# Attention's token sums moved into the slots of the convolution norm, and two plain projection slots turned into seven-product slots

## The reference, cut to what matters

```python
n = rms_norm_2(h, mix_norm_g[l])
proj = n @ w_in[l]                       # q k v, index heads, xr, yg, cv (2 x 1024), gt (3 x 1024)
attn = dsa_attention(q, k, v, qi, ki, wi)
rnn  = rg_lru_branch(xr, yg, ...)
cnv  = silu(layer_norm(causal_depthwise_conv(a * sigmoid(g), dw_w, dw_b), ln_g, ln_b))   # 31 taps
g_attn, g_rnn, g_conv = split(sigmoid(gt), 3)
merged = g_attn * (attn @ w_o_attn) + g_rnn * (rnn @ w_o_rnn) + g_conv * (cnv @ w_o_conv)
h = h + merged @ w_out
# then the feed-forward half of the layer
```

## Time and profile before

| | |
|---|---|
| timed runs | 1715.67, 1718.28, 1719.57 us; median 1718.28 us |
| profiled execution | 1715.31 us, span 1713.5 us, mean granted TensorE clock 0.989 |
| busy share of the span | PE 97%, PEld 86%, DVE 66%, POOL 39%, ACT 32% |
| DVE busy from 700 to 800, 1200 to 1300, 1300 to 1400 us | 81%, 88%, 91% |
| slots 34 to 45, first layer | about 767 to 855 us |
| slots 34 to 45, second layer | about 1389 to 1474 us |

### The profile page before, as it was taken

The page is one execution under the profiler, slowest core; times in us unless marked ns, Lnnn a source line. Parts: engine busy times, 40 slices in busy tenths (PEclk is TensorE's granted clock), DMA queues, the critical chain, the costliest instruction groups (busy, mean ns, idle before and its releaser), DMA issues.

```text
span 1713.5 us, 36091 instructions
## 1 busy us (share of the span) xinstructions
PE 1662.7 (97%) x14758; PEld 1475.4 (86%) x14758; DVE 1136.8 (66%) x2047; ACT 556.5 (32%) x1255; POOL 660.5 (39%) x581
## 2 busy tenths in 40 slices
PE   5999998999999999999999999999999999999999
PEld 3777657999889988878889999989888889999999
DVE  5647155665378889995757664368888977576743
ACT  3233463444343444424130100233554314220100
POOL 1534103553045342114636554165122027446552
PEclk9999996999999999999999999999999999999999
DMA  9333200000544434333435444543343343444543
GB/s 383 117 113 123 74 1 2 4 4 4 199 147 136 160 124 148 124 122 124 151 121 197 152 163 160 166 148 126 125 171 124 135 150 131 160 164 170 173 160 111
DMA packets 53379, 225.71 MB, mean 132 GB/s; under 512 B 5088, under 2 KB 29024, under 8 KB 29280
## 3 DMA queue, kind: packets, MB, share of 16 engines
q1 hardware_dynamic: 53216, 223.40, 37.4%
HBM read 222.34 MB, written 1.05 MB: 130 GB/s over the span
## 4 chain that ended last, share of the span: by engine, by line
PE 86%; DVE 7%; ACT 2%; DVEq 2%; DMA 1%; issue 1%; ACTq 0%; SPq 0%
PE PS L742 17%; PE PS L785 17%; PE PS L1052 15%; PE PS L1076 8%; PE PS L2552 5%; PE PS L2664 3%; DVE arena L1474 2%; PE PS L2073 2%; PE PS L2086 2%; PE PS L724 1%; PE PS L2761 1%; PE PS L902 1%; PE PS L865 1%; PE PS L1016 1%; DMA ring<-stream_dram 1%
## 5 line engine op out<-in xcount | busy, mean ns | idle before, releaser
L785 PE MATMUL PS<-arena,ring 128*128 128x272 f32 (+1 forms) x1600 | 374.1, 388 | 0.9 <-DVE arena L1698 0.5
L785 PEld LDWEIGHTS PS<-arena,ring 128*128 128x128 f32 x1600 | 298.8, 190 | 57.9 <-issue 7.0
L1918 POOL TENSOR_TENSOR arena<-ring 128x512 f32<-128x512 f32 x50 | 72.5, 1449 | 447.2 <-DMA ring<-stream_dram 397.1
L1474 DVE SCALAR_TENSOR_TENSOR arena<-arena,par 128x272 f32<-128x272 f32 (+1 forms) x480 | 236.3, 550 | 7.3 <-issue 0.4
L742 PE MATMUL PS<-arena,ring 128*128 128x136 f32 (+1 forms) x1600 | 209.6, 279 | 2.3 <-ACT arena L1162 2.0
L742 PEld LDWEIGHTS PS<-arena,ring 128*128 128x128 f32 x1600 | 199.6, 190 | 9.6 <-ACT arena L1162 2.8
L742 PE MATMUL PS<-arena 128*128 128x136 f32 (+1 forms) x1200 | 155.5, 281 | 4.4 <-DVE arena L1579 3.9
L1052 PE MATMUL PS<-arena 128*128 128x136 f32 (+1 forms) x1280 | 152.1, 277 | 0.0
L742 PEld LDWEIGHTS PS<-arena 128*128 128x128 f32 x1200 | 146.8, 192 | 6.0 <-DVE arena L1735 2.6
L1052 PEld LDWEIGHTS PS<-arena 128*128 128x128 f32 x1280 | 148.7, 191 | 0.0
L1052 PE MATMUL PS<-arena,ring 128*128 128x136 f32 (+1 forms) x960 | 116.1, 277 | 0.0
(11 more groups left out here) (416 smaller groups left out, 2950.5 us busy)
## 6 DMA issues: line engine op xcount, KB each, us to landing
ring<-stream_dram SPq DMA_DIRECT2D x185, 1024.0 KB, 4.9
ring<-stream_dram SPq DMA_DIRECT2D x32, 512.0 KB, 4.3
ring<-stream_dram SPq DMA_DIRECT2D x16, 384.0 KB, 3.5
arena<-x_dram SPq DMA_DIRECT2D x1, 2048.0 KB, 8.3
cst<-const_dram SPq DMA_DIRECT2D x1, 1080.0 KB, 6.7
out_dram<-H SPq DMA_DIRECT2D x4, 256.0 KB, 3.8
cst<-const_dram SPq DMA_DIRECT2D x1, 912.0 KB, 12.2
arena<-stream_dram SPq DMA_DIRECT2D x1, 512.0 KB, 11.1
```

The lines of the kernel that those rows point to most:

```text
L785: last = mm(PS[:, 2 * (j % 2) + f, nw], w[:, k, P * f:P * f + P], src[:, k, nw], start=k == 0, stop=k == KD - 1)
L1474: stt(CVG[:, c, NQ], CVA[:, c, j + Q0:j + T2], dw_w[l][:, c, j:j + 1], CVG[:, c, NQ], ALU.mult, ALU.add)
L1918: g.tensor_tensor(to[:, 0], w21, w22, ALU.add).then_inc(L["summed"], 1)
```

## The change

`CONV_SUM_J` becomes 35 in both layers, and `ATT_SUM_J` 36. Slots 36 and 37 are added to `MIXED`. The four attention sums are split: two in VectorE's slot 36 and two in its slot 37, behind the links of the norm chain that now stand there, and TensorE's waits for them are split likewise. In the first layer the one convolution step of slot 35 goes to slot 34. The norm chain starts one slot earlier in the first layer and two in the second; the attention sums come one slot later in the first and three in the second.

```diff
-CONV_SUM_J, ATT_SUM_J = (36, 37), (35, 33)
+CONV_SUM_J, ATT_SUM_J = 35, 36
-MIXED = [*range(2, 8), 9, 11, 12, 15, 18, 21, 24, 27, 35, *range(OA_J, OC_J + 3), *range(WO_J + 1, MIXES)]
+MIXED = [*range(2, 8), 9, 11, 12, 15, 18, 21, 24, 27, 35, 36, 37, *range(OA_J, OC_J + 3), *range(WO_J + 1, MIXES)]
...
-              for late in ({27: 4, 28: 8, 29: 3, 30: 7, 31: 5, 32: 3, 33: 4, 34: 4, 35: 1},
+              for late in ({27: 4, 28: 8, 29: 3, 30: 7, 31: 5, 32: 3, 33: 4, 34: 5},
...
                     product_g(j)
...
+                    if j == OA_J:
+                        pe.wait_ge(L["att_halves"], B["att_halves"] + 3)
...
                     product_c(j)
+                    if j == OA_J + 1:
+                        pe.wait_ge(L["att_halves"], B["att_halves"] + 4)
...
-                if j == ATT_SUM_J[l]:
+                if j == ATT_SUM_J:
                     dve.wait_ge(L["o_kept"], B["o_kept"] + len(R))
-                    x = AT.rearrange("p (k e) t -> p k e t", e=2)
-                    token_sums(v, x[:, :, 0], x[:, :, 1], TATT, n0, n1).then_inc(L["att_halves"], 1)
+                    tt(sums[0], even[..., n1], even[..., n0], ALU.subtract).then_inc(L["att_halves"], 1)
+                    tt(sums[2], odd[..., n1], even[..., n1], ALU.subtract).then_inc(L["att_halves"], 1)
+                if j == ATT_SUM_J + 1:
+                    dr()
+                    tt(sums[1], odd[..., n1], sums[0], ALU.subtract).then_inc(L["att_halves"], 1)
+                    dr()
+                    tt(sums[3], odd[..., n0], sums[1], ALU.subtract).then_inc(L["att_halves"], 1)
```

More of the change, by code:

```diff
@@ L1291, in scalar_layers @@
                     copy_a(j)
-                    if j == CONV_SUM_J[l] + 1:
+                    if j == CONV_SUM_J + 1:
                         square(0)
-                    if j == CONV_SUM_J[l] + 4:
+                    if j == CONV_SUM_J + 4:
                         conv_silu(1).then_inc(L["conv_out"], 1)
@@ L1397, in scalar_layers @@
                     open_branch(GTS[0][:, 4:8, NQ], GTC_J + 4, True)
-                if j == CONV_SUM_J[l] + 1 and j not in MIXED:
+                if j == CONV_SUM_J + 1 and j not in MIXED:
                     square(0)
                     square(1).then_inc(L["conv_sq"], 1)
-                if j == CONV_SUM_J[l] + 2:
+                if j == CONV_SUM_J + 2:
                     act.wait_ge(L["conv_sq_sum"], B["conv_sq_sum"] + 1)
                     inverse_root(TQ[:, 0, NQ], PS[:, 5, NQ], D, L["conv_root"])
-                if j == CONV_SUM_J[l] + 3:
+                if j == CONV_SUM_J + 3:
                     conv_silu(0)
@@ L1710, in vector_layers @@
             done = 0
+            heads_of = AT.rearrange("p (k e) t -> p k e t", e=2)
+            even, odd, sums = heads_of[:, :, 0], heads_of[:, :, 1], [TATT[:, i, :, 0:nh] for i in range(4)]
             for j in range(1, WO_J):
@@ L1719, in vector_layers @@
                         ).then_inc(L["conv_cent"], 1)
-                if j == CONV_SUM_J[l] + 2:
+                if j == CONV_SUM_J + 2:
                     dve.wait_ge(L["conv_sq"], B["conv_sq"] + 1)
                     add_tiles(v, CSUM[:, 1, NQ], CSQ[:, :, NQ], CSQ[:, 0:4, NQ]).then_inc(L["conv_sq_in"], 1)
-                if j == CONV_SUM_J[l] + 3:
+                if j == CONV_SUM_J + 3:
                     dve.wait_ge(L["conv_root"], B["conv_root"] + 1)
                     tt(CVG[:, :, NQ], CVG[:, :, NQ], over(TQ[:, 0, NQ], 8), ALU.mult).then_inc(L["conv_normed"], 1)
-                if j == CONV_SUM_J[l] + 4:
+                if j == CONV_SUM_J + 4:
                     dve.wait_ge(L["conv_out"], B["conv_out"] + 1)
                     x = CVG.rearrange("p (k e) t -> p k e t", e=2)
-                    even, odd, to = x[:, :, 0], x[:, :, 1], [TCNV[:, i, :, 0:nh] for i in range(4)]
-                    tt(to[0], even[..., n1], even[..., n0], ALU.subtract).then_inc(L["conv_halves"], 1)
-                    dr()
-                    tt(to[1], odd[..., n1], to[0], ALU.subtract).then_inc(L["conv_halves"], 1)
-                    tt(to[2], odd[..., n1], even[..., n1], ALU.subtract).then_inc(L["conv_halves"], 1)
+                    to = [TCNV[:, i, :, 0:nh] for i in range(4)]
+                    tt(to[0], x[:, :, 0, n1], x[:, :, 0, n0], ALU.subtract).then_inc(L["conv_halves"], 1)
+                    dr()
+                    tt(to[1], x[:, :, 1, n1], to[0], ALU.subtract).then_inc(L["conv_halves"], 1)
+                    tt(to[2], x[:, :, 1, n1], x[:, :, 0, n1], ALU.subtract).then_inc(L["conv_halves"], 1)
                     dr()
-                    tt(to[3], odd[..., n0], to[1], ALU.subtract).then_inc(L["conv_halves"], 1)
+                    tt(to[3], x[:, :, 1, n0], to[1], ALU.subtract).then_inc(L["conv_halves"], 1)
                 if j - 1 in MIXED:
```

12 lines of the change are left out of this document (6 added, 6 removed).

## The result

| | before | changed |
|---|---|---|
| median of 20 runs each | 1716.30 us | 1722.49 us |
| lowest to highest | 1709.19 to 1719.57 | 1718.07 to 1727.69 |
| profiled execution, span | 1715.31, 1713.5 | 1721.45, 1719.6 |
| ratio with 95% interval | | 1.0042 [1.0032, 1.0051] |

The account below looks back on a forecast made before the run. TensorE was taken to bound the kernel (86% of the chain). Products -2.53, old waits and slow clock -8.00, new waits +5.8 and +8.6, clock +1.2 gave +5.1, taken as +4.8: 1723.1 us, 8-in-10 range 1717.0 to 1727.5.

Parts of the forecast that it names:

- GpSimd's sums on the taps: GpSimd's new sums for slot 36 each hold up one VectorE tap, by 1.04 us, delaying what TensorE wants.
- the sigmoid in the norm chain: Last sigmoid waits for slot 37's sum_f1 and needs table loads, delaying Silu and slot 39's copy: 6.1 us of work.
- Products, -2.53: Halving slots 36 and 37 saves 0.84 us a slot in the first layer and 0.84 for both in the second.
- Old waits and slow clock, -8.00: TensorE's waits of 2.42 and 3.93 us in the two layers, and 1.65 of slow clock, all go.
- New waits, 14.4 forecast: TensorE's new waits: first layer 1.1 + 3.3 + 1.4 us, second 2.6 + 1.5 + 3.2 + 1.3.
- The 3.3: First layer: TensorE waits 3.3 us at product c of slot 39 for a ScalarE copy behind sigmoid and Silu.
- Slot 34, 2.6 forecast: Second layer: two GpSimd sums hold taps ahead of slot 32's gate, so slot 34's wait grows from 0.54 to 2.6 us.
- The clock, +1.2 forecast: TensorE runs slower behind the new wait at c of slot 39: 0.6 us a layer, ends 0 and 1.7.
- the clock takes its full price: Rival, chance 0.11: full half-rate cost in both layers, perhaps at the 2.6 us waits too: +2.2 to +4, 1726.5 us.
- The norm's sum in the second layer, 1.5 forecast: Slot 35, second layer: VectorE's sums ready at 1402.5, wanted by TensorE at 1401.0, a wait of 1.5 us.
- d of slot 38 in the second layer, 1.3 forecast: Second layer: the second Silu group holds copy_e, so TensorE waits 1.3 us more at d of slot 38.
- Slots 40 to 42 without a wait: Slots 40 to 42 lose their waits of 1.50 and 2.45 us, since slot 42's sums are made at least a slot earlier.

Follow-up runs that it names:

- The repeat: The unchanged kernel before, profiled once more for a second profile: 1712.03 us, one run.
- three waits filled: Changed kernel with useless TensorE products ahead of c of slot 39, slot 34 (second layer) and d of slot 38: 1712.24 us, one run.
- two waits filled: Changed kernel with useless TensorE products ahead of c of slot 39 and of slot 34 in the second layer: 1717.13 us, 1.0015 to before.
- the kernel with the chain alone: Changed kernel with slots 36 and 37 plain again, only norm chain and attention sums moved: 1718.09 us, 1.0019 to before.
- the fastest: Changed kernel, GpSimd's slot 36 sums held back, last sigmoid behind second Silu group, token sums split over two slots: 1704.91 us, 0.9950 to before.
- both, token sums behind: Changed kernel, GpSimd's slot 36 sums held back, sigmoid behind Silu, sum_f0 ahead of token sums, copy_e ahead of second Silu: 1712.01 us, 0.9994 to before.

## Why the prediction was right, and where it was wrong

The mechanism was right: the old waits went, and two new causes, GpSimd's sums on the taps and the sigmoid in the norm chain, cost more than the products save. That the time, 1722.49, lies 0.6 us from the forecast is partly luck: before's median was 1718.28 when I forecast and 1716.30 over 20 runs. The difference is the thing to judge: +4.8 forecast, +7.2 by the ratio, +6.6 in the stretches.

- **Products, -2.53.** Right: 6.49 us a slot, and the first layer of the kernel with mixed slots alone gained 1.6 of 1.7.
- **Old waits and slow clock, -8.00.** All old waits went or changed. But 1.65 of it was half rate that before shows only in some executions. The repeat says 6.3.
- **New waits, 14.4 forecast, 10.5 measured** (1.02, 2.43, 1.02; 3.51, 0, 2.32, 0.17). In the first layer 1.1 was 1.02, with the sums ready at the forecast place. The 3.3 was 2.43, with the sigmoid's load starting at the forecast place (802.8, less the 1.8 by which this profile is earlier, is 801.0; measured 800.93). The 0.6 us of hold for the normalisation did not come, GpSimd was held in its stead, but it started 0.5 later. What was less comes behind it: the 0.4 for held small sums is nothing, and the rows below are 0.3 shorter:

```profile
797.15 2.41 DVE L1731 TENSOR_TENSOR arena<-arena 128x2176 f32<-128x2176 f32 x1
797.22 3.47 POOL L1931 TENSOR_TENSOR arena<-arena,ring 128x512 f32<-128x512 f32 x1 [0.16 <-issue]
...
800.93 1.28 ACT L1225 ACT_TABLE_LOAD   x1 [0.59 <-DVE arena L1591]
...
802.22 1.11 ACT L1225 ACTIVATE arena<-arena 128x1088 f32<-128x1088 f32 x1
...
803.35 1.28 ACT L1280 ACT_TABLE_LOAD   x1
...
804.64 2.13 ACT L1280 ACTIVATE arena<-arena,par 128x272 f32<-128x272 f32 x4
...
806.68 0.26 ACT L1146 ACTIVATE arena<-PS 128x136 f32<-128x136 f32 x1
```

  From the sigmoid's load to the end of the first Silu group it is 5.8 us (6.1 forecast), and the copy that product c wants follows at once. The order was read rightly; that a mixed slot 37 is needed for it was not (1.91 without).
- **Slot 34, 2.6 forecast, 3.51 measured.** I left the gate at before's 1388.16 and counted the sums that start ahead of it. But a held tap moves the gate, and so another sum falls ahead of it. Seven sums met the twelve taps, for four in the earlier trace rows:

```profile
1380.27 12.11 DVE L1478 SCALAR_TENSOR_TENSOR arena<-arena,par 128x256 f32<-128x256 f32 x12
...
1392.46 0.69 DVE L1702 TENSOR_TENSOR arena<-PS,arena 128x512 f32<-128x512 f32 x1
```

  (12.11 - 5.00) / 7 = 1.02 us each, so the price of 1.04 held. By the Trainium skill's exclusive lock (SBUF — State Buffer, SBUF: two separate sides) each tap could lose the sum's whole 1.3; the mean here is again below it.
- **The clock, +1.2 forecast, 4.8 to 6.3 measured** with the waits filled, 7.5 by the length of the slow rows (of which some hides other waits). This is the step that failed, the term with the largest error: "I take 0.6 us a layer". I let it apply to slot 39 alone, thought most of it hidden behind ScalarE, and did not put it on slot 34, whose wait I had at 2.6 and where nothing is hidden. The rival *the clock takes its full price* named the mechanism, and even its +2.2 to +4 was short. Its point of decision, "about 2.45", was too high: half rate also followed 2.32 us in both profiles of the changed kernel and 1.96 with slots 36 and 37 plain.
- **The norm's sum in the second layer, 1.5 forecast: 0.** The cause is the sum of GpSimd that fell ahead of slot 32's gate. The taps of slot 33 then lost only 0.24 us (4.05 for 3.81) of the 2.1 I had put there, so VectorE's sums were ready 0.9 earlier than forecast, and TensorE, held longer at slot 34, wanted them some 0.7 later. The slow clock isn't needed for it: with three waits filled and the clock full, the sums are ready at 1397.29 and TensorE's row has no wait either:

```profile
1397.44 0.67 PE L708 MATMUL PS<-arena,c 128*128 128x256 f32 x2
```

- **d of slot 38 in the second layer, 1.3 forecast: 0.17.** Here the slow clock paid: product c at half rate lasts until the copy for d is nearly there. With c at full rate (two waits filled) the wait was 1.00. I had taken 0.3 us for such overlap.
- **The sum.** Two errors of opposite sign, -4 on waits and +4 to +6 on the clock, made a sum that looks better than its parts. That they nearly cancel is luck in the main.
- **Slots 40 to 42 without a wait:** right, until the sigmoid is put right.

By terms the measured sum is -2.5 - 8.0 + 10.5 + 7.5 = +7.5 against +6.6 in the stretches; the rest of 0.9 is not resolved.

## What to carry to other kernels

Count a wait of TensorE of some 2 us or more twice, once for itself and once for what runs at half rate behind it (fifteen of sixteen such waits here), and ask whether a short wait follows; filling it with useless products shows at once how much of it is the clock. When an engine's work is held by another's, let the wanted time move too before counting what falls ahead of it. And where links of a chain are moved past other work on an in-order engine, the bill is in what then stands between them: here a sigmoid with two table loads, and moving that one instruction back, with GpSimd's sums held for one link and the token sums split, turned 0.42% slower into 0.50% faster.

## What was not expected of the hardware

**An addition caught behind GpSimd, 1.2 us far behind the change.** Every kernel with slots 36 and 37 mixed has a longer tail: 244.4 to 244.6 us behind the second stretch, against 243.1 to 243.2 for before, its repeat and the kernel with the chain alone. The place is the feed-forward norm's last addition in the second layer. Timelines of before and of the changed kernel:

```profile
1501.58 2.92 DVE L1813 TENSOR_TENSOR arena<-arena 128x256 f32<-128x256 f32 x6
...
1504.19 1.44 POOL L1441 TENSOR_TENSOR arena<-ring 128x512 f32<-128x512 f32 x1 [12.89 <-PE PS L1008]
1504.56 0.70 PE L708 MATMUL PS<-arena,c 128*128 128x256 f32 x2 [0.46 <-DVE arena L1813]
```

```profile
1506.44 2.43 DVE L1824 TENSOR_TENSOR arena<-arena 128x256 f32<-128x256 f32 x5
...
1509.04 1.26 POOL L1445 TENSOR_TENSOR arena<-ring 128x512 f32<-128x512 f32 x1 [12.91 <-PE PS L1012]
1509.29 1.30 DVE L1824 TENSOR_TENSOR arena<-arena 128x256 f32<-128x256 f32 x1 [0.42 <-issue]
...
1510.64 0.70 PE L708 MATMUL PS<-arena,c 128*128 128x256 f32 x2 [1.68 <-DVE arena L1824]
```

The sixth addition and a GpSimd instruction start within 0.3 us of each other. Before, the addition was in first (its row ends at 1504.50); in the changed kernel GpSimd is, the addition takes 1.30 us for 0.43, and TensorE waits 1.68 for 0.46, as in all ten other kernels and repeats with mixed slots. Why the mixed slots, 100 us earlier, decide this race was not tried. With it the profiles agree with the timed ratios: 7.9 us or 0.46% for the changed kernel, -9.3 + 1.2 = -8.1 or -0.47% for the fastest. Of the others one lies outside its interval: "both, token sums behind", -3.1 us or -0.18% for [-0.16, +0.05].

**The length of one wait doesn't decide the half rate alone.** 2.40 us of idleness left the clock full in before's repeat; 2.45 was followed by 0.52 in its first profile, and 2.40 by 0.50 in the changed kernel's repeat. In the stretches of all fourteen profiles sixteen waits lasted 1.9 us or more, and half rate came behind fifteen, for two of them only behind the next wait (1.91 and 2.43, each with 1.02 behind it). Behind a single shorter wait, up to 1.88, it never came; behind 0.66 and 1.02 us, two microseconds apart, it did (0.53), behind 0.54 and 1.00 not. The Trainium skill (TensorE: Matmul & The Clock Gate, Part 1) has half rate after idleness, and all these windows agree with that level; when it comes, the runs here show only as told.
